# FFN gate and up with a 512-column matmul for the high weight part, adaLN items spread over nine stages, and the a buffers 32 bytes further on

## The reference

```python
m = c_act @ w + b                      # 1024 x 3072 for each stage
shift, scale, gate = jnp.split(m, 3, axis=-1)
h = rmsnorm(x, g) * (1.0 + scale) + shift
x = x + 0.5 * gate * swiglu(h, w_gate, w_up, w_down)       # ffn
def swiglu(h, w_gate, w_up, w_down):
    return (jax.nn.silu(h @ w_gate) * (h @ w_up)) @ w_down
def conv_ffn(h, w_up, conv_w, conv_b, w_down):             # cffn
    u = h @ w_up
    ...   # causal convolution over 3 tokens for each column, plus bias
    gate, val = jnp.split(y, 2, axis=-1)
    return (jax.nn.silu(gate) * val) @ w_down
```

## Time and profile before

| | |
|---|---|
| median of 3 runs | 1892.75 us |
| lowest, highest | 1885.89, 1894.99 us |
| the profiled execution | 1896.41 us, its span 1894.6 us |
| mean granted TensorE clock | 0.982 |
| busy: PE, PE loads, DVE, ACT | 95%, 92%, 76%, 51% |
| matmuls | 14,644 |
| HBM traffic | 427 MB, mean 225 GB/s |

### The profile page before, as it was taken

How to read it: one execution, slowest core, us unless ns; L and a number is a source line. 1 busy time by engine, 2 the same in 40 slices (tenths; PEclk the granted TensorE clock), 3 DMA queues, 4 the chain that set the end, 5 groups by cost and what they waited for, 6 DMA issues and landing times.

```text
span 1894.6 us, 34144 instructions
## 1 busy us (share of the span) xinstructions
PE 1795.6 (95%) x14644; PEld 1737.1 (92%) x14644; DVE 1445.1 (76%) x1716; ACT 961.7 (51%) x1256; POOL 0.2 (0%) x4
## 2 busy tenths in 40 slices
PE   2998999999999999999989999898999999989999
PEld 2998989998999999999979999897999988979999
DVE  7799877877789878976548897655898667447666
ACT  3433456666543454346564444555644555666553
POOL 0000000000000000000000000000000000000000
PEclk9999999999999999999999999999999998999999
DMA  9998824343599759973426996232485544324551
GB/s 399 417 366 340 300 109 156 135 177 134 187 380 365 309 218 371 361 296 130 178 101 262 347 393 250 109 140 109 175 320 192 181 142 161 118 90 162 193 180 42
DMA packets 67278, 426.11 MB, mean 225 GB/s; under 512 B 7264, under 2 KB 10352, under 8 KB 30448
## 3 DMA queue, kind: packets, MB, share of 16 engines
q1 hardware_dynamic: 63216, 415.21, 57.9%
q10 hardware_dynamic: 3968, 9.63, 1.5%
HBM read 423.74 MB, written 3.17 MB: 225 GB/s over the span
## 4 chain that ended last, share of the span: by engine, by line
PE 85%; DVE 10%; ACT 3%; issue 1%; DMA 1%; SPq 0%; DVEq 0%; ACTq 0%
PE bank L1365 24%; PE bank L1367 24%; PE bank L1366 24%; DVE w_lo L816 3%; PE bank L1423 2%; DVE macc L847 2%; DMA modws<-mods 1%; PE bank L1687 1%; PE bank L1378 1%; PE bank L1380 1%; DVE mix L1002 1%; PE bank L1385 1%; PE bank L1529 1%; PE bank L1668 1%; PE bank L1564 0%
## 5 line engine op out<-in xcount | busy, mean ns | idle before, releaser
L1365 PE MATMUL bank<-h_hi,w_hi 128*128 128x256 f32 x2864 | 810.4, 283 | 14.0 <-DVE w_lo L816 12.3
L1366 PE MATMUL bank<-h_lo,w_hi 128*128 128x256 f32 x2864 | 804.4, 281 | 0.0
L1367 PE MATMUL bank<-h_hi,w_lo 128*128 128x256 f32 x2864 | 804.2, 281 | 0.0
L816 DVE TENSOR_TENSOR w_lo<-raw,w_hi 128x2048 fp32r<-128x2048 f32 x277 | 633.4, 2288 | 128.1 <-ACT w_hi L420 127.6
L420 ACT ACTIVATE w_hi<-raw 128x2048 fp32r<-128x2048 f32 x277 | 529.3, 1911 | 155.8 <-PE bank L1367 144.5
L1365 PEld LDWEIGHTS bank<-h_hi,w_hi 128*128 128x128 f32 x2864 | 543.8, 190 | 19.5 <-DVE w_lo L816 15.1
L1366 PEld LDWEIGHTS bank<-h_lo,w_hi 128*128 128x128 f32 x2864 | 546.7, 191 | 0.2
L1367 PEld LDWEIGHTS bank<-h_hi,w_lo 128*128 128x128 f32 x2864 | 545.3, 190 | 0.0
L1365 PE MATMUL bank<-a_hi,w_hi 128*128 128x256 f32 x1280 | 362.4, 283 | 3.1 <-DVE a_lo L1244 3.1
L1366 PE MATMUL bank<-a_lo,w_hi 128*128 128x256 f32 x1280 | 359.6, 281 | 0.0
L1367 PE MATMUL bank<-a_hi,w_lo 128*128 128x256 f32 x1280 | 359.2, 281 | 0.0
(11 more groups left out here) (250 smaller groups left out, 1692.4 us busy)
## 6 DMA issues: line engine op xcount, KB each, us to landing
raw<-weights SPq DMA_DIRECT2D x277, 1024.0 KB, 4.9
modws<-mods SPq DMA_DIRECT2D x144, 768.0 KB, 6.5
mix<-mods SPq DMA_DIRECT2D x6, 1024.0 KB, 8.1
mix<-mods ACTq DMA_DIRECT2D x8, 512.0 KB, 10.3
modws<-mods SPq DMA_DIRECT2D x2, 1024.0 KB, 12.1
biases<-scratch ACTq DMA_DIRECT2D x1, 2048.0 KB, 12.2
mix<-biases ACTq DMA_DIRECT2D x4, 512.0 KB, 4.2
par<-params ACTq DMA_DIRECT2D x1, 1189.0 KB, 8.3
```

The costliest lines, as they stand in the source:

```text
L816: eng.tensor_tensor(w_lo[g % NW][:, :], raw[g % NRAW][:, :], w_hi[g % NW][:, :], ALU.subtract).then_inc(sems["wlo"], 1)
L1365: eng.matmul(dst, ah, bh, start=start, stop=False, skip_group_check=skip)
L1366: eng.matmul(dst, ah, bl, start=False, stop=False, skip_group_check=skip)
L1367: return eng.matmul(dst, al, bh, start=False, stop=stop, skip_group_check=skip)
```

## The change

Three edits.

1. h_hi and h_lo become one buffer `h`, 128 x 8 x 2 x 256, so that the high and the low part of a tile lie side by side. In gate and up blocks of ffn and cffn (`gemm_wide`) w_hi meets both in one matmul of 512 columns, which fills a bank: the first 256 columns hold the high product, the last 256 the low one. w_lo times h_hi (256 columns) is added to the first half. A block takes two banks (gate 4 and 5, up 6 and 7), for the two halves of hidden columns. The first block of a stage keeps its order, with three matmuls. The two halves of a bank are added later: ACT copies the low half to SBUF (`glo`, `ulo`), DVE adds the high half from the bank (`gad`, `uad`). silu, the product, and in cffn the taps, then read SBUF.
2. The 180 items are put in nine stages by the list `SPOTS` (27, 13, 30, 30, 12, 30, 12, 14, 12), at most one a block in ffn and cffn. A job's transposes go into the ring of `modws` buffers (18 users a job instead of 16) instead of `mix`.
3. `small` grows from 4 to 12 columns. So acg, a_hi, a_lo and mix start 32 bytes further on. a_hi started at byte 198176 of a partition, which is 32 past a multiple of 64; h_hi starts at 109120, a multiple of 64.

```diff
+FFN_SPOTS = list(range(2, 3 * NFB - 1))
+SPOTS = [FFN_SPOTS[3:], even([4 * i + b for i in range(1, 8) for b in (-1, 2)], 13), FFN_SPOTS, FFN_SPOTS,
+         [1, 2, 2] + [4 * i + b for i in range(1, 4) for b in (0, 1, 2)], FFN_SPOTS,
+         [1, 1, 2] + [4 * i + b for i in range(1, 4) for b in (0, 0, 1)],
+         even(FFN_SPOTS, 14), [0, 0, 0, 1, 4, 4, 7, 7, 10, 10, 13, 13], []]
...
-        h_hi = sb("h_hi", [P, KT, T], F32R)
-        h_lo = sb("h_lo", [P, KT, T], F32R)
+        h = sb("h", [P, KT, 2, T], F32R)
+        h_hi, h_lo = h[:, :, 0, :], h[:, :, 1, :]
...
-        small = sb("small", [P, 4])
+        small = sb("small", [P, 12])
...
+            def gemm_wide(n, st, i=0, a=0, b=0, first=False):
...
+                    for part, d in both:
+                        for kk in range(KT):
+                            eng.matmul(d, hi[:, kk, part], h[:, kk, :, :].rearrange("p a t -> p (a t)"), start=kk == 0,
+                                       stop=kk == KT - 1, skip_group_check=True)
+                            mm = eng.matmul(d[:, 0:T], lo[:, kk, part], h_hi[:, kk, :], start=False, stop=kk == KT - 1,
+                                            skip_group_check=True)
...
                 def gate(i, a, b):
                     split(st, i, a, b)
                     eng.wait_ge(sems["blk"], k.block(st, i, a, b) + 1)
-                    k.wait("mul", st, i, 1, -1)
-                    k.inc("silu", eng.activation(sg, bank[4][:, :].rearrange("p (a t) -> p a t", a=2), ACT.Silu))
+                    k.wait("silu", st, i, 1, -1)
+                    k.inc("glo", eng.activation(cg, halves(4)[1], ACT.Copy))
 
                 def up(i, a, b):
                     split(st, i, a, b)
+                    k.wait("gad", st, i, 1, 0)
+                    k.wait("mul", st, i, 1, -1)
+                    k.inc("silu", eng.activation(sg, cg, ACT.Silu))
+                    eng.wait_ge(sems["blk"], k.block(st, i, a, b) + 1)
+                    k.inc("ulo", eng.activation(cu, halves(6)[1], ACT.Copy))
...
                 def up(i, a, b):
+                    k.wait("glo", st, i, 1, 0)
+                    k.inc("gad", eng.tensor_tensor(cg, halves(4)[0], cg, ALU.add))
                     split(st, i, a, b)
-                    eng.wait_ge(sems["blk"], k.block(st, i, a, b) + 1)
+                    k.wait("ulo", st, i, 1, 0)
+                    k.inc("uad", eng.tensor_tensor(cu, halves(6)[0], cu, ALU.add))
+                    k.wait("uad", st, i, 1, 0)
                     k.wait("silu", st, i, 1, 0)
                     k.wait("alo", st, i, 1, -1)
-                    k.inc("mul", eng.tensor_tensor(act, sg, bank[5][:, :].rearrange("p (a t) -> p a t", a=2),
-                                                   ALU.mult))
+                    k.inc("mul", eng.tensor_tensor(act, sg, cu, ALU.mult))
...
                 def gate(i, a, b, first=False):
                     if not first:
-                        k.wait(free4, st, i, per4, -per4)
-                    gemm(bank[4], st, i, a, b, first=first)
+                        k.wait("gad", st, i, 1, -1)
+                    gemm_wide(4, st, i, a, b, first=first)
```

More of the change, by code:

```diff
@@ L35 @@
 GATE_AT = 1
-MODS_OF = {0: (1, 2), 2: (3, 4), 3: (5, 6), 5: (7, 8), 7: (9,)}
-MODS_STEP = {"gate": 2, "up": 1, "down": 1}
 AHEAD = 2
@@ L107, in constants, with even, items, user @@
     return out
[L110 to L120 removed]
+PIECES = 16
+FOLDS = 4
+ITEMS = PIECES + FOLDS
+USERS = PIECES + 2
+def even(spots, n):
+    return [spots[k * len(spots) // n] for k in range(n)]
+FFN_SPOTS = list(range(2, 3 * NFB - 1))
[3 more added lines that the diff above has]
+         even(FFN_SPOTS, 14), [0, 0, 0, 1, 4, 4, 7, 7, 10, 10, 13, 13], []]
+def items(st, b):
+    first = sum(len(x) for x in SPOTS[:st])
+    return [((first + k) // ITEMS + 1, (first + k) % ITEMS) for k, at in enumerate(SPOTS[st]) if at == b]
+def user(job, k):
+    return USERS * (job - 1) + (k if k < PIECES else PIECES + (k - PIECES) % 2)
+def mod_loads(u):
+    return sum(1 for v in range(u % 4, u + 1, 4) if v % USERS < PIECES)
 class Plan:
@@ L150, in steps @@
         if kind in ("ffn", "cffn"):
-            out |= {"silu": g, "mul": g, "ahi": g, "alo": g}
+            out |= {"silu": g, "mul": g, "ahi": g, "alo": g, "glo": g, "gad": g, "ulo": g, "uad": g}
         if kind == "cffn":
@@ L285, in build, with halves @@
         eps_c, eps128_c, one_c = small[:, 0:1], small[:, 1:2], small[:, 2:3]
+        def halves(n):
+            return [psum[:, n:n + 2, r * T:(r + 1) * T] for r in range(2)]
         def acc(m):
@@ L374, in _ @@
                     load(plan.first[st] + b + AHEAD + NRAW)
-                    if kind in ("ffn", "cffn") and b >= 2:
-                        for q in mod_parts(st, (b + 1) // 3, ("gate", "up", "down")[(b + 1) % 3]):
-                            load_mod(q + 4)
+                    for job, n in items(st, b):
+                        if n < PIECES or n >= PIECES + 2:
+                            load_mod(user(job, n) + 4)
             for m in range(KT):
@@ L489, in taps @@
                 def taps(i, up):
-                    b, dst = bank[5 if up else 4], cu if up else cg
+                    src, dst = (uu, cu) if up else (ug, cg)
+                    k.wait("uad" if up else "gad", st, i, 1, 0)
                     k.wait("mul", st, i, 1, -1)
@@ L501, in gate @@
                     eng.wait_ge(sems["blk"], k.block(st, i, a, b) + 1)
+                    k.wait("tap2", st, i, 2, -2)
+                    k.inc("glo", eng.activation(ug, halves(4)[1], ACT.Copy))
                     taps(i, 0)
@@ L508, in up @@
                     eng.wait_ge(sems["blk"], k.block(st, i, a, b) + 1)
+                    k.wait("tap2", st, i, 2, -1)
+                    k.inc("ulo", eng.activation(uu, halves(6)[1], ACT.Copy))
                     taps(i, 1)
@@ L1008, in gate @@
                     split(st, i, a, b)
+                    k.wait("glo", st, i, 1, 0)
+                    k.inc("gad", eng.tensor_tensor(ug, halves(4)[0], ug, ALU.add))
                     taps(i, 0)
@@ L1012, in up @@
                     split(st, i, a, b)
+                    k.wait("ulo", st, i, 1, 0)
+                    k.inc("uad", eng.tensor_tensor(uu, halves(6)[0], uu, ALU.add))
                     taps(i, 1)
@@ L1270, in body @@
                         finish(i, h)
+                    gather(st, a * i + b + (1 if kind == "dsa" else 2) + more)
                 if kind == "dsa":
```

120 lines of the change are left out of this document (71 added, 49 removed).

## The result

| | before | after |
|---|---|---|
| median | 1892.88 us | 1908.08 us |
| lowest, highest | 1885.89, 1894.99 us | 1906.68, 1912.92 us |
| profiled execution, its span | 1896.41, 1894.6 us | 1906.68, 1904.7 us |

The ratio is 1.0099, 95% interval 1.0072 to 1.0125. The time is outside the range (1840 to 1884) and on the other side of no change. That is a loss of some 15 to 19 us, by the medians or by the ratio.

What follows compares the result with a forecast made beforehand. The prediction took TensorE, busy 95% of 1894.6 us, as the bound, its weight loads setting the pace. Terms 35 + 6 - 3 + 4 - 2 - 9 = 31 us, off the median 1892.75, gave 1862 us, range 1840 to 1884.

Steps and rivals of the forecast that it cites:

- part 1: Gate and up blocks: a wide and a narrow matmul take 331 ns for a triple's 340 or 353, saving 35 us.
- R2: Rival: matmul overhead goes with columns, not loads, so the wide one costs twice a narrow one; 1897 us, chance 0.05.
- R4: Rival: f32r streams slower beyond 256 columns, at 0.97 ns a column +500 us; decides from 235 ns, chance 0.03.
- R1: Rival: both matmul rhythms end at the lower spacing, giving 1846 us; chance 0.10.
- 2, the a buffers: Down blocks: a buffers moved to a multiple of 64 bytes save 6 us, bounds 0 and 15.
- 3, evacuation: ACT copies and DVE adds: hidden in FFN, 11 us lost in the stage at 1335 us; net -3.
- 5, stage ends: Ends of FFN and cffn stages: low part of z comes late, together -9 us, bounds -3 and -14.
- 4, items: Items spread: +4 us in the first stage, 2 us charged in the mixer stages.
- R3: Rival: DVE sets the end of FFN and cffn iterations, 1928 us; chance 0.13, of which 0.06 slower.

Runs made afterwards that it cites:

- e5: The changed kernel with the wide matmul cut into two of 256 columns again, all else as it is: 1899.69 us, ratio 1.0033 to the kernel before.
- e1: The kernel before with groups of 24 float32r matmuls of several widths, loads and addresses behind its end: 113.3 ns at 256 columns, 233.3 at 512.
- e8: The kernel before with groups of 24 float32r matmuls, some with odd members, behind its end: 113.3 ns ahead of a lone 512-column one, 117.8 behind.
- e11: The changed kernel with the item products of the stage at 1337 us cut to 32 columns: 1901.2 us, ratio 1.0054 to the kernel before.
- e4: The kernel before with the shift of the a buffers alone (small at 12 columns): 1870.32 us, ratio 0.9887.
- e7: The kernel before with 32 unused bytes ahead of h_hi, so that h and not a lies 32 past a multiple of 64: 1899.43 us, ratio 1.0031.
- e10: The changed kernel without the shift, small keeping its 4 columns: 1913.53 us, ratio 1.0132 to the kernel before.
- e6: The kernel before with items spread and a buffers shifted, without wide matmul, copies and adds: 1875.81 us, ratio 0.9906.
- e3: The kernel before with the spreading of the items alone: 1870.92 us, ratio 0.9922.

## Why the prediction was wrong

**The step that failed is the first term of part 1**: "The pair should cost 216 for the wide one plus 113.4 to 117.8 for the narrow one". It cost 235 + 118 in the kernel, 353 together. Forecast was a gain of 35 us, measured a loss of 12 (e5 against the changed kernel). Two inferences led there. From 8 columns taking 111.8 and 256 taking 113.4 ns I read that the load sets both; e1 shows that it doesn't set the second (half a load, no less time). And the 216 of the earlier trace rows is a row of float32, as the 216 of the zeroing is one of bf16; a float32r stream of 512 columns takes 233.3. The earlier trace rows had the one float32r row above 256 columns; the stream of 160 ns that I read out of it for 384 columns was near the 173.3 of e1, but a load and a drain stood around it, and it priced no stream. No trace of before has wide float32r matmuls one behind the other.

**R2 is what happened to the matmuls**: the overhead goes with the columns and the wide one costs twice a narrow one, 2 x 117.8 = 235.6. I gave it 0.05. Its time of 1897 came out lower than the 1908 for what follows. The Trainium skill, TensorE: Matmul & The Clock Gate, section Back-to-back issue gap, gives 215.8 ns for 512 columns by its formula. (It gives the formula for an isolated matmul; I had read it as one whose load is hidden.) The zeroing in bf16 agrees (216). e1 and the kernel measured 233 to 235, so for float32r streams the measurement decides against the formula; but the gain of 5 us that I had worked out from it for the whole merging was nearer than my 35. R4 named 235 ns as the point from which it decides; that value came, but at 0.469 ns a column, not 0.97.

**R1, inverted.** I left the rhythm open ("nothing says which rhythm settles"). e8 shows that a wide matmul moves the stream to the higher spacing, and in the changed kernel no merged block is at the lower one. So the pair is never cheaper than the dear triple, and the stages that had the lower spacing lose it, down blocks included. The spread of executions fits: 6 us for the changed kernel (4 runs) and 5 for e11 (10 runs, with the wide matmul too), 21 us for e5 (12 runs). My 24 of 63 iterations at the lower spacing was the draw of one execution: in the traces of e1 and e8 the stage at 486 us of the same kernel is at the higher one, 152.7 us for the nine iterations that took 148.69.

```profile
511.25:663.97 152.72, 152.72 (x1298) 152.72 (x1297) 135.07 (x83) 60.86 (x45) 0.00 (x0) 1.00 0.90 347
```

**2, the a buffers.** The mechanism was right: a runs as h does when both lie at a multiple of 64 (e4), and the slow value goes with the address (e7). Its size depends on the company: some 6 us in the changed kernel (e10 against it) and 1.1% alone, part of which may be the draw of the spacings. That 6 was the forecast value too is luck: it came from FFN stages at the lower spacing, with down blocks at 5.44 us, and the changed kernel has none of these; its down blocks take 5.66, and of the 6 us between e10 and it the two traces have 5.9 in the mixer stages. The 16-byte rule of the Trainium skill, SBUF — State Buffer, section Door 1: The DMA port swizzle, does not carry over to PE's reads: e1 has 113.3 and 118.6 ns at addresses 32 bytes apart.

**3, evacuation.** In ffn stages it is hidden as forecast: DVE is busy 128.5 us of nine iterations, 14.3 each (15.1 forecast), PE idle nowhere. In stage 7 the mean, 160.6 / 9 = 17.8, is the 17.7 of the forecast by luck: four iterations take PE's own 16.96, and four are 1.5 to 2.8 us longer. Against e6, at the same spacing, the nine lost 8.0 us and the entry 0.8, where 11 were forecast. Mis-sized was the end.

**5, stage ends.** ffn: 1.3 us late at 667.37, forecast 1.4. Last stage: the end is 1.2 us longer than in e6, as forecast (its entry and first iterations lost 2.0 more, mostly in waits for w_lo, which I hadn't forecast). Stage 7: forecast 2.5, measured 7.5 (23.7 against 16.2 in e6). I costed the end as if DVE came to it on time. Its add began at 1528.14, 3.7 us after the copy could be ready (1523.81 + 0.60), since in that stage DVE is behind: PE waits for a w_lo in about half the iterations. Of the 7.5 us some 5 are the longer wait, and the rest is the matmuls on z at the clock of 0.50. In all, copies and adds cost 24 us where parts 3 and 5 had 20: 11 in the iterations of stage 7 and 9 at the ends. (Part 3's net of 3 has in it the 7.9 us that the spreading saves, and e6 has those already.)

**4, items.** The iteration of 22.58 us is gone. The 2 us for the mixer stages are not shown either way: in e3 stages 1, 4, 6 and 8 take 248.9, 128.5, 143.5 and 159.4 us, and the kernel before in the traces of e1 and e8 248.8 and 246.4, 128.3 and 129.0, 144.0 and 143.3, 159.1 and 159.5. e3 has -15 us in all; by parts 3 and 4 it would have been some 10 (7.9 of waits in stage 7, 4 in stage 0, less 2).

R3 did not come in ffn stages. In stage 7 alone it did: DVE sets about half of the iterations and the end there, some 16 us against e6.

**In sum.** The forecast was 35 us from the wide matmul, 16 from spread and shift (10 and 6) and -20 from copies and adds: 31. The runs have -12, +18 and -24. All but 2 us of the miss is the wide matmul.

**What stays open.** Why a lone matmul of 384 columns brings the lower spacing (three places) and one of 512 the higher (one place, and every merged block), as did one of 128 (one place); the runs show only that. What sets the spacing at a stage's start: it differs between executions of one kernel. How the 6.9 us that stay in stage 7 without the items' time arise. And how much of the 0.9887 of e4 is the address and how much its draw.

## What to carry to other kernels

Before merging matmuls, measure a stream of the merged shape in the same type: two limits can have the same value at one size and be different things. A row of another type or another pass count is no price: here 512 columns take 216 ns in bf16 and 233 in float32r. Where an engine works in order and is behind, its lateness is paid at the stage's end at full price, so cost an end from the time at which the engine arrives, not from the block's. And where executions of one kernel scatter by 1%, look for two spacings of the same instruction before crediting an edit: here 60 matmuls whose results nobody reads were worth as much as spread and shift together (0.9% each).

## What was not expected of the hardware

- float32r matmuls with 128x128 loads: 111.7 ns at 128 columns, 113.3 at 256, 173.3 at 384, 233.3 at 512, at a granted clock of 1.00. bf16 with 512 columns: 216.
- 256 columns have two spacings, 113.3 and 117.8 ns, kept over hundreds of matmuls. A rest can change it (36 of 59 at the lower behind one, in the last two stages in turn). A lone 384-column matmul moved the stream to the lower in the three places where it met the higher, and left it there in 57; a lone 512-column one moved it to the higher.
- The moving operand 32 bytes past a multiple of 64: 118.3 to 118.6 ns at 256 columns (117.3 to 118.7 for a in the kernel before), no difference at 512.
- A wait of PE for its own last matmul costs 0.5 us.
